# Expert rows scattered by GpSimd, LayerNorm sums on VectorE and stationary time-step weights in a one-core decoder step

## What is computed

```python
h = _rmsnorm(x, norm_mix_g) * (1 + sc1) + sh1
z, xbc, dt_raw, glu_in, gate_ssd, gate_conf = _split(h @ w_in, IN_SPLITS)
dt = softplus(dt_raw + ssd_dt_bias)                    # 32 columns of w_in
u = u_a * sigmoid(u_g)                                 # glu_in
v, cconv_new = _causal_dwconv(u, cconv0, conf_conv_w, conf_conv_b)   # width 31
v = silu(_layernorm(v, conf_ln_g, conf_ln_b))          # over the 2048 channels
conf_branch = v @ w_conf_out
...
# 32 experts, D_FF 256; each token goes to 2 of them
out = einsum('tef,efd->td', silu(h2 @ w_gate) * (h2 @ w_up) * gate, w_down)
x = x + g2 * out
```

## Time and profile before

| | |
|---|---|
| median of 3 runs | 2205.31 us (2201.94 to 2205.66) |
| time of the profiled execution | 2203.45 us |
| its span | 2201.7 us |
| TensorE busy (matmuls) | 1960.4 us, 89% of the span |
| VectorE, ScalarE, GpSimd busy | 670.6, 315.1, 23.8 us |
| moved by DMA | 526.31 MB, of it 33.51 MB written to HBM |
| mean granted clock | 0.943 |

### The profile page before, as it was taken

One profiled execution on the slowest core, in us unless ns is written; L12 is line 12 of the kernel. 1 busy time (PEld: TensorE's weight loads), 2 busy tenths in 40 slices (PEclk: granted clock), 3 DMA queues, 4 the chain that ended last, 5 costly groups with the idle time before them and its releaser, 6 DMA issues.

```text
span 2201.7 us, 31937 instructions
## 1 busy us (share of the span) xinstructions
PE 1960.4 (89%) x12929; PEld 1447.6 (66%) x12929; DVE 670.6 (30%) x1698; ACT 315.1 (14%) x723; POOL 23.8 (1%) x53
## 2 busy tenths in 40 slices
PE   5689999999999999999999999999878777777881
PEld 3357777777777777777677767777666454555560
DVE  3016877870120023340455541110231111111115
ACT  1321010101230000001222230000230000000112
POOL 0000000000000000000000000000000000000000
PEclk9679999999999999999999999999779999999995
DMA  8996546556645544344665573454568999999994
GB/s 225 344 330 214 190 158 216 168 188 200 196 159 191 166 141 151 117 152 112 188 180 180 170 240 115 153 191 157 193 264 364 428 426 429 425 428 427 426 413 149
DMA packets 334477, 526.31 MB, mean 239 GB/s; under 512 B 17565, under 2 KB 311285, under 8 KB 315381
## 3 DMA queue, kind: packets, MB, share of 16 engines
q1 hardware_dynamic: 321101, 490.42, 63.1%
q10 hardware_dynamic: 11794, 22.75, 3.0%
q0 software_dynamic: 1472, 11.67, 1.4%
HBM read 492.99 MB, written 33.51 MB: 239 GB/s over the span
## 4 chain that ended last, share of the span: by engine, by line
PE 75%; DMA 15%; SPq 5%; DVE 3%; ACT 1%; issue 1%; ACTq 0%; DVEq 0%; POOL 0%; POOLq 0%
PE bank L1055 48%; DMA ring<-in_w_exp_down 7%; PE bank L1224 6%; DMA ring<-in_w_exp_up 5%; PE bank L1367 5%; SPq L393 5%; PE bank L1379 3%; PE bank L1062 2%; PE bank L1077 2%; PE bank L1237 1%; DMA ring<-in_w_ada 1%; PE bank L1219 1%; DMA ring<-in_w_exp_gate 1%; PE bank L1309 1%; PE bank L1360 0%
## 5 line engine op out<-in xcount | busy, mean ns | idle before, releaser
L1055 PE MATMUL bank<-hT,ring 128*128 128x288 f32 x2816 | 694.5, 409 | 3.1 <-DVE hT L1517 3.1
L1055 PEld LDWEIGHTS bank<-hT,ring 128*128 128x128 f32 x2816 | 535.3, 191 | 156.0 <-issue 9.7
L1055 PE MATMUL bank<-work,ring 128*128 128x288 f32 x1536 | 378.7, 408 | 3.8 <-DVEq L1809 2.4
L1055 PEld LDWEIGHTS bank<-work,ring 128*128 128x128 f32 x1536 | 290.9, 190 | 87.6 <-issue 3.4
L1367 PE MATMUL bank<-ring,hT 128*64 128x128 f32 x4096 | 239.1, 275 | 42.1 <-DMA ring<-in_w_exp_up 21.7
L1367 PEld LDWEIGHTS bank<-ring,hT 128*64 128x64 f32 x4096 | 225.8, 138 | 68.2 <-issue 36.0
L1379 PE MATMUL bank<-ring,work 128*64 128x512 f32 x512 | 140.3, 699 | 55.5 <-DMA ring<-in_w_exp_down 54.6
L705 ACT ACTIVATE work<-bank 9x256 f32<-9x256 f32 x192 | 72.1, 376 | 430.1 <-PE bank L1062 428.4
L1062 PE MATMUL bank<-ring,work 128*9 128x256 f32 x1536 | 110.6, 437 | 24.4 <-DMA ring<-in_w_ada 23.3
L1224 PE MATMUL bank<-hT,ring 128*128 128x288 f32 x512 | 128.6, 410 | 0.0
L1379 PEld LDWEIGHTS bank<-ring,work 128*64 128x64 f32 x512 | 40.0, 157 | 133.1 <-issue 72.7
(11 more groups left out here) (347 smaller groups left out, 1208.4 us busy)
## 6 DMA issues: line engine op xcount, KB each, us to landing
ring<-in_w_in SPq DMA_DIRECT2D x52, 2048.0 KB, 8.9
ring<-in_w_ada SPq DMA_DIRECT2D x48, 2048.0 KB, 11.3
ring<-in_w_exp_gate SPq DMA_DIRECT2D x32, 2048.0 KB, 15.3
ring<-in_w_exp_up SPq DMA_DIRECT2D x32, 2048.0 KB, 16.9
ring<-in_w_exp_down SPq DMA_DIRECT2D x32, 2048.0 KB, 17.9
ring<-in_w_conf_out SPq DMA_DIRECT2D x8, 2048.0 KB, 11.4
ring<-in_w_ssd_out SPq DMA_DIRECT2D x8, 2048.0 KB, 8.4
ring<-in_w_o SPq DMA_DIRECT2D x8, 2048.0 KB, 9.0
```

Of the source, the lines that this page charges most:

```text
L1055: mm = nc.tensor.matmul(bank[b][:, 0:T], ring[:, s, kk, j * P:(j + 1) * P], rhs[:, kk], start=(kk == 0), stop=(kk == KC - 1))
```

## The change

Three things are changed.

1. *Expert rows.* ScalarE issues no writes any more. GpSimd issues one indirect DMA per expert (128 partitions of 4 KB) with a table of row numbers `put_i`, one column for each expert: a filled place goes to its own row of `expert_rows` (now 576 rows in sorted order, seen as 1152 halves), and a place that no pair fills gets a number beyond `bounds_check` and is left out. A buffer `ysb` is handed back by GpSimd (`ysb_free`), after it has issued the next expert's DMA and the buffer's own has landed.
2. *LayerNorm sums.* VectorE adds the 16 chunks of `vb`, and later of the squares, with one `tensor_reduce` each; TensorE multiplies the one resulting 128 x 288 tile with ones. These two matmuls stand ahead of units 5 and 8 of `gc`, each with a wait for VectorE, and the squares, root and SiLU move on ScalarE from `z1` into `gc`.
3. *Time steps.* `wdt` is stationary (32 columns), `hT` moves (288 columns), four groups side by side as in an `a` unit; the matmuls stand ahead of unit 2 of `z1`. A second small matmul (ahead of unit 6) adds the four groups and turns them, with `unstack`, a matrix that GpSimd now makes at the start and that was a product of `stack` before. SyncE loads `wdt` ahead of `z1`'s first units.

```diff
@@ -437,12 +441,11 @@
                 sp.dma_start(cconv_s[0, b, CK - 1 - NL:CK - 1],
                              tailrow[CK - 1 + NL * b:CK - 1 + NL * (b + 1)]).then_inc(S["tail_out"], 16)
 
-            stream("z1", rest=False)
             sp.wait_ge(S["vsamp_ready"], 1)
             sp.wait_ge(S["conv_ready"], 1)
             sp.wait_ge(bank_free[7], use("tail", 7))
             sp.dma_start(wdt, w_in[:, :, DT0:DT0 + H], allow_slow_non_contiguous=True).then_inc(S["wdt_loaded"], 16)
-            stream("z1", head=False)
+            stream("z1")
             stream("co", rest=False)
 
...
@@ -631,10 +647,19 @@
                                           staged[j], 16)
 
             gp.wait_ge(S["yi_ready"], 1)
+            for e in range(NE):
+                gp.wait_ge(S["kept_low"], e + 3)
+                gp.wait_ge(S["kept_high"], e + 3)
+                gp.indirect_dma_start(out=y_halves, out_offset=bass.IndirectOffsetOnAxis(ap=put_i[:, e:e + 1], axis=0),
+                                      in_=ysb[:, e % 2], in_offset=None, bounds_check=4 * T - 1, oob_is_err=False).then_inc(
+                                          y_out[e % 2], 16)
+                if e:
+                    gp.wait_ge(y_out[(e - 1) % 2], 16 * ((e - 1) // 2 + 1))
+                    gp.sem_inc(S["ysb_free"], 1)
             gp.wait_ge(S["moe_done"], 1)
             for q, (t0, rows) in enumerate(TOK):
...
@@ -773,18 +797,22 @@
                 ac.sem_inc(bank_free[4 + q], 1)
                 ac.sem_inc(S["tail_rows"], 1)
             ac.wait_ge(S["part_zero"], 2)
-            walk("gc", part_mix, to_buffer("gc", gb, ACT.Sigmoid))
+            def layer_norm(u):
+                if u == 6:
+                    square(vb, sq_ln, ("centred", 1))
+                if u == 9:
+                    root(2)
+                    for c in range(KC):
+                        if c % 4 == 0:
+                            ac.wait_ge(S["v_ready"], c // 4 + 1)
+                        ac.activation(vb[:, c], vb[:, c], ACT.Silu, bias=LN_B[:, c:c + 1], scale=LN_G[:, c:c + 1]).then_inc(
+                            S["vb_free"], 1)
+
+            walk("gc", part_mix, to_buffer("gc", gb, ACT.Sigmoid), before=layer_norm)
 
             ac.wait_ge(S["tail_out"], 128)
             ac.wait_ge(S["out_done"], 16)
-            square(vb, sq_ln, ("centred", 1))
             walk("z1", part_mix, to_buffer("z1", zb, ACT.Silu))
-            root(2)
-            for c in range(KC):
-                if c % 4 == 0:
-                    ac.wait_ge(S["v_ready"], c // 4 + 1)
-                ac.activation(vb[:, c], vb[:, c], ACT.Silu, bias=LN_B[:, c:c + 1], scale=LN_G[:, c:c + 1]).then_inc(
-                    S["vb_free"], 1)
...
@@ -921,16 +949,11 @@
                     ac.wait_ge(S["gu_done"], 1)
                     ac.activation(sil[:, 0], bank[4][:, 0:P], ACT.Silu).then_inc(S["sil_ready"], 1)
 
-            def keep_rows(e, par, n, pair):
-
-                ac.wait_ge(y_out[par], pair * 32 + 32)
+            def keep_rows(par, n):
+
+                ac.wait_ge(S["ysb_free"], n + 1)
                 ac.wait_ge(S["d0_done"], n + 1)
                 ac.activation(ysb[:, par, 0:512], bank[2 * par][:], ACT.Copy).then_inc(S["kept_low"], 1)
-                ac.wait_ge(S["kept_low"], n + 3)
-                ac.wait_ge(S["kept_high"], n + 3)
-                for half in range(2):
-                    ac.dma_start(y_one[ds(e, 1), :, D // 2 * half:D // 2 * (half + 1)].rearrange("e s n -> (e s) n"),
-                                 ysb[WIN * half:WIN * (half + 1), par]).then_inc(y_out[par], 16)
 
...
@@ -1127,20 +1150,46 @@
                 for n in range(4):
                     mm = nc.tensor.transpose(bank[4 + q][0:CK - 1 + NS, n * P:(n + 1) * P], utail[:, 4 * q + n], ident[:])
                 mm.then_inc(bank_ready[4 + q], 1)
-            project("gc", hT)
-            pe.wait_ge(S["conv_ready"], 1)
-            pe.wait_ge(S["vsamp_ready"], 1)
-            ones_sum("ln", vb, 4, range(KC))
-            project("z1", hT)
-            ones_sum("lnsq", sq_ln, 5, range(KC), squares=4)
-
-            pe.wait_ge(S["wdt_loaded"], 16)
-            fill("dt", 6)
-            for q, (t0, rows) in enumerate(TOK):
-                for k in range(KC):
-                    mm = nc.tensor.matmul(bank[6][0:rows, H * q:H * (q + 1)], hT[:, k, t0:t0 + rows], wdt[:, k],
-                                          start=(k == 0), stop=(k == KC - 1))
-            mm.then_inc(bank_ready[6], 1)
+            def norm_sums(u):
+
+                if u == 5:
+                    pe.wait_ge(S["sums_in"], 1)
+                    pe.wait_ge(bank_free[6], use("gc", 6, 0))
+                    nc.tensor.matmul(bank[6][:, SUM0:SUM0 + T], ones[:], stat[:], start=True, stop=True).then_inc(S["sums_done"], 1)
+                if u == 8:
+                    pe.wait_ge(S["sums_read"], 1)
+                    pe.wait_ge(S["sums_in"], 2)
+                    pe.wait_ge(bank_free[7], use("gc", 7, 0))
+                    nc.tensor.matmul(bank[7][:, SUM0:SUM0 + T], ones[:], stat[:], start=True, stop=True).then_inc(
+                        S["sums_done"], 1)
+                if u == 11:
+                    pe.wait_ge(S["sums_read"], 2)
+
+            project("gc", hT, before=norm_sums)
+
+            def time_steps(u):
+
+                if u == 2:
+                    pe.wait_ge(S["wdt_loaded"], 16)
+                    pe.wait_ge(bank_free[5], use("gc", 5, 1))
+                    for k in range(KC):
+                        q = k % 4
+                        mm = nc.tensor.matmul(bank[5][H * q:H * (q + 1), 0:T], wdt[:, k], hT[:, k], start=(k < 4),
+                                              stop=(k >= KC - 4))
+                    mm.then_inc(S["sums_done"], 1)
+                if u == 3:
+                    pe.wait_ge(S["sums_in"], 3)
+                if u == 6:
+                    pe.wait_ge(S["unstack_ready"], 1)
+                    pe.wait_ge(bank_free[7], use("z1", 7, 0))
+                    for q, (t0, rows) in enumerate(TOK):
+                        mm = nc.tensor.matmul(bank[7][0:rows, SUM0 + H * q:SUM0 + H * (q + 1)], dt_part[:, t0:t0 + rows],
+                                              unstack[:], start=True, stop=True)
+                    mm.then_inc(S["sums_done"], 1)
+                if u == 7:
+                    pe.wait_ge(S["sums_read"], 3)
...
@@ -1574,27 +1622,37 @@
                 dve.link(ve, ve.tensor_tensor(acc_s, acc_s, tmpc, ALU.add))
             ve.tensor_copy(vb[:, :, NP:T], acc_s).then_inc(S["vsamp_ready"], 1)
 
-            take("ln", 4)
-            dve.link(ve, ve.tensor_scalar(stat[:], bank[4][:, 0:T], 1.0 / D, None, ALU.mult))
-            ve.sem_inc(bank_free[4], 1)
             ve.wait_ge(S["vsamp_ready"], 1)
+            ve.tensor_reduce(stat[:], vb.rearrange("p k t -> p t k"), AX_X, ALU.add).then_inc(S["sums_in"], 1)
+            ve.wait_ge(S["sums_done"], 1)
+            dve.link(ve, ve.tensor_scalar(stat[:], bank[6][:, SUM0:SUM0 + T], 1.0 / D, None, ALU.mult))
+            ve.sem_inc(S["sums_read"], 1)
             for q in range(4):
                 v_ = vb[:, 4 * q:4 * q + 4]
                 dve.mark(ve.tensor_tensor(v_, v_, stat[:].unsqueeze(1).broadcast_to([P, 4, T]), ALU.subtract))
                 dve.wait(ve)
                 ve.sem_inc(S["centred"], 1)
-            inv_rms("lnsq", 5, 2, D)
+            ve.wait_ge(S["squares_ready"], 8)
+            ve.tensor_reduce(stat[:], sq_ln.rearrange("p k t -> p t k"), AX_X, ALU.add).then_inc(S["sums_in"], 1)
+            ve.wait_ge(S["sums_done"], 2)
+            ve.tensor_scalar(stat[:], bank[7][:, SUM0:SUM0 + T], 1.0 / D, EPS, ALU.mult, ALU.add).then_inc(S["mean_ready"], 1)
+            ve.wait_ge(S["root_ready"], 2)
+            ve.sem_inc(S["sums_read"], 1)
+            dve.link(ve, ve.reciprocal(rs[:], rs[:]))
             for q in range(4):
                 v_ = vb[:, 4 * q:4 * q + 4]
                 ve.tensor_tensor(v_, v_, rs[:].unsqueeze(1).broadcast_to([P, 4, T]), ALU.mult).then_inc(S["v_ready"], 1)
 
 
-            take("dt", 6)
...
-            dve.link(ve, ve.scalar_tensor_tensor(out=first_row, in0=iota_e, scalar=float(WIN), in1=bank[3][:, 96:128],
-                                                 op0=ALU.mult, op1=ALU.subtract))
+            put, spare = small[0][:, 0], small[0][:, 1]
+            dve.mark(ve.tensor_scalar(put, bank[3][:, 96:128], 2.0, slot2, ALU.mult, ALU.add))
+            dve.link(ve, ve.tensor_scalar(spare, bank[3][:, 128:160], slot1, None, ALU.is_le))
             ve.sem_inc(bank_free[3], 1)
-            dve.link(ve, ve.tensor_scalar(first_row, first_row, fits, None, ALU.mult))
-            dve.link(ve, ve.tensor_tensor(pos, pos, first_row.unsqueeze(1).broadcast_to([P, 3, NE]), ALU.add))
+            dve.link(ve, ve.scalar_tensor_tensor(out=put, in0=spare, scalar=4096.0, in1=put, op0=ALU.mult, op1=ALU.add))
+            dve.link(ve, ve.tensor_copy(put_i, put))
...
```

69 lines of the change are left out of this document (43 added, 26 removed).

## The result

The changed kernel took a median of **2185.03 us** (2183.43 to 2186.60), the kernel before 2205.30 (2201.94 to 2205.66) beside it on the same chip. The ratio is 0.9914, interval [0.9901, 0.9926]: 16 to 22 us faster. The forecast was 2185, its range 2175 to 2195.

The account below looks back on a forecast made before the run. TensorE bounds the kernel before about 1600 us, bytes moved bound the experts' stage. 2203.45 + 2.6 (sums, time steps) - 22.5 (expert rows) = 2183.6 us, plus 1.9 for the median: 2185 us, range 2175 to 2195.

Parts of the forecast that it names:

- The bound: Whole kernel: before about 1600 us TensorE's work and waits count one to one; in the experts' stage bytes count.
- Part 1, the wait: First ones matmul in `gc`: TensorE waits 24.2 us (23.4 to 29.1) for VectorE's reduction, itself 5.8 us (5.0 to 10.7).
- The clock: Behind TensorE's wait in `gc`: a few us at half clock, 2.0 us lost (between 1 and 4).
- The hidden second sum: Ones matmul ahead of unit 8 of `gc`: no wait of TensorE, cover 8 us, 3 at the reduction's upper rate.
- Part 2: Time steps: 10.4 us taken away, 2.15 and 0.65 us of products added, 1.0 us of clock in `co`'s first unit saved.
- Parts 1 and 2 together: LayerNorm sums and time steps, before the experts: savings eaten by one wait, +2.6 us in all.
- Part 3: Expert rows: 0.38 MB less written saves 0.9 us a step, 19.8 us over 22 steps; -22.5 us in all.
- C: Rival, expert writes: unfilled places cost their time all the same, expert part gives nothing, 2208 us; chance 0.05.
- A: Rival, experts' stage: queues exceed 427 GB/s without the writes (437) and late steps gain too, 2178 us; chance 0.14.
- B: Rival: reduction at upper rate (+5 us), half the expert gain lost (+11), 2190, 2196 or about 2194 us; chance 0.12.
- D: Rival, hand-back through GpSimd: one scattered write holds it longer than 11 us, delaying every step; 2245 us at 13; chance 0.03.

Follow-up runs that it names:

- late_sums: Changed kernel with the two ones matmuls moved from before units 5 and 8 of `gc` to before 8 and 11: 2157.03 us, ratio 0.9796.
- write_few: Changed kernel with ScalarE's plain transfers of the first 16 rows of each half in place of the indirect write: 15.085 us a step, 2169.00 us (one run).
- sums_only: Kernel before with only the LayerNorm sums and time steps changed, expert rows as before: 2205.12 us, ratio 1.0005.
- rows_only: Kernel before with only the indirect write of the expert rows, sums and time steps as before: 2182.48 us, ratio 0.9918.
- scatter_all: Changed kernel with every place written, unfilled ones to rows of their own, 0.524 MB a step: 15.955 us a step, 2204.73 us (one run).

## Why the prediction was right, and where not

- **The bound.** TensorE one to one before the experts, bytes in them: shown by `late_sums` (26.1 us of wait and 2.9 of clock removed, 28.0 us gained in the medians, 28.3 by expert 0's copy) and by `write_few`.
- **Part 1, the wait.** The mechanism held. The size was off by the reduction ("= 5.8 us"): 7.86 us. My working gave 1.05 ns an element and 2.9 ns a result from short rows; it was 1.71 ns an element, inside the bounds but nearer to the strided row. The clock cost 2.9, not 2.0, and 1.4 to 2.9 in the kernels with the same wait; my bounds were 1 and 4. The hidden second sum was hidden.
- **Part 2.** The products took 2.12 and 0.81 us (forecast 2.15 and 0.65). The step that failed is "the granted clock fell in the old form's second half ... 1.0 us more goes". In the changed kernel the time steps are gone from there and `co`'s first unit took 17.41 us, longer than before. In seven other kernels without them it took 15.77, and the 1.0 us came. So the term can't be counted on; whether the low clock of the kernel before belonged to its time steps stays open.
- **Parts 1 and 2 together**, +2.6: +6.2 by the start of `co`, +2.1 in the time (`sums_only`). In the changed kernel 3.0 us came back between the wait of 2.24 us and the end of `gs`'s first unit (17.7 us before, 14.7 after), which runs at full clock, and 1.7 in the sum of ones near 1559 us (9.69 us before, 8.00 after), neither of which I had forecast. By expert 0's copy 0.7 us is left. That the total is near 2185 is luck: the first half came out 1.9 us better than my +2.6, the second 4.5 worse than my -22.5, and the 1.9 us that I added for a median above the profiled execution did not come (2185.03 against 2185.59).
- **Part 3.** The step that failed is "0.38 MB less ... I take 0.9". It holds for `write_few` (15.085), not for the filled places of a window, which always fall on the same engines first. 0.51 us a step came. Of the 8.6 us missing in 22 steps, the first two steps, the last two and the end made up 5.6; the five steps between cost 1.5 more. In all 18.0 us between the two profiles and 20.5 in `rows_only` (about 18 by its ratio), forecast 22.5.
- **The rivals.** C's kernel was run (`scatter_all`): had the places been written, the time would be 2204.7 (one run). A's 437 GB/s did not come, not even without any expert write (426). B was partly right: the reduction took 2 of the 5 us that it allowed, and the steps gave less than the bytes promise, though for a reason that it did not name. D did not come.

## What to carry to other kernels

A matmul that waits for another engine belongs where its operand is surely there, not where it is first allowed: ask when the producer ends, count the units until then, and put it behind them. When a transfer is made smaller by leaving rows out, ask which rows stay: here the time went by the fullest transfer engine, and rows at the front of a window sit on few. And a term of 2 or 3 us of clock behind a wait could not be forecast here: the same short wait cost 1.6 us or nothing, and the same wait of 26.1 us cost 1.4 to 2.9.

## What was not expected of the hardware

- A skipped place of an indirect transfer still makes a packet of 4 bytes (9 ns); 128 of them and 16 more cost 0.09 us of a step that is bound by transfers (one run each with and without).
- Eight rows of 4 KB cost 0.23 or 0.54 us a step, by their partitions.
- VectorE's strided reduction of 4608 numbers to 288 took 7.86 to 8.21 us, four contiguous additions 5.2.
